# An expert stream fed in wider transfers: a loop over experts 4 to 29, and the drain for extra passes moved into their branch

## What is computed

```
g_prob  = softmax(xt @ w_group + b_group);  one group of 4
e_w     = the two best of the 8 experts of that group, renormalised
y       = (silu(xb @ w_gate[e]) * (xb @ w_up[e])) @ w_down[e]     for each of 32 experts, on its tokens
out     = sum over the two experts of each token of weight * y
```

## Time and profile before

| what | value |
|---|---|
| median of three runs | 1237.26 us |
| the profiled execution | 1237.28 us, span 1235.5 us |
| mixer and routing | until about 306 us |
| experts | 306 to 1218 us |
| TensorE busy | 931.6 us, 75% |
| DMA | 462.33 MB, mean 374 GB/s over the span |

### The profile page before, as it was taken

One profiled execution on the slowest core, in us unless ns is written; L12 is line 12 of the kernel. 1 busy time (PEld: TensorE's weight loads), 2 busy tenths in 40 slices (PEclk: granted clock), 3 DMA queues, 4 the chain that ended last, 5 costly groups with the idle time before them and its releaser, 6 DMA issues.

```text
span 1235.5 us, 17448 instructions
## 1 busy us (share of the span) xinstructions
PE 931.6 (75%) x7799; PEld 526.0 (43%) x7799; DVE 378.8 (31%) x480; ACT 223.3 (18%) x381; POOL 28.4 (2%) x60
## 2 busy tenths in 40 slices
PE   9999999999976666676666663866766766766774
PEld 7788788886433333333232321323333323323331
DVE  5454745444222222222222113222222222222214
ACT  6544555443100000000000000100000000000003
POOL 1100000000100000000000000000000000000003
PEclk9999999999988778878887876987788788787787
DMA  8877567858999999999999999999999999999993
GB/s 283 318 268 244 177 218 279 282 169 300 370 426 427 426 428 426 429 425 427 426 426 428 426 428 424 428 426 428 426 428 424 430 425 427 428 427 427 427 413 123
DMA packets 57083, 462.33 MB, mean 374 GB/s; under 512 B 5000, under 2 KB 5616, under 8 KB 31664
## 3 DMA queue, kind: packets, MB, share of 16 engines
q1 hardware_dynamic: 56272, 458.25, 90.7%
q0 software_dynamic: 656, 2.94, 0.7%
q10 hardware_dynamic: 80, 0.02, 0.0%
HBM read 459.09 MB, written 2.10 MB: 373 GB/s over the span
## 4 chain that ended last, share of the span: by engine, by line
DMA 55%; PE 40%; ACT 2%; DVE 2%; POOL 1%; issue 1%; POOLq 0%; ACTq 0%; DVEq 0%
DMA slot<-in_e_w_up 54%; PE scattered_out L1072 20%; PE bank L1261 8%; PE bank L1286 5%; PE bank L1234 2%; PE scattered_out L1299 1%; PE bank L1243 1%; ACT arena L594 1%; POOL h L426 1%; PE bank L1127 1%; DVE w_lo L693 0%; PE bank L1173 0%; ACT w_hi L440 0%; DVE acc L939 0%; DMA arena<-in_a_b_s 0%
## 5 line engine op out<-in xcount | busy, mean ns | idle before, releaser
L1261 PE MATMUL bank<-slot,arena 128*32 128x256 f32 x4064 | 340.4, 507 | 250.7 <-DMA slot<-in_e_w_up 249.5
L1261 PEld LDWEIGHTS bank<-slot,arena 128*32 128x32 f32 x4064 | 183.1, 144 | 417.4 <-issue 385.2
L939 DVE TENSOR_TENSOR acc<-scattered_out,acc 128x2048 f32<-128x2048 f32 x60 | 137.5, 2292 | 637.1 <-PE scattered_out L1299 637.1
L693 DVE TENSOR_TENSOR w_lo<-w_raw,w_hi 128x1024 fp32r<-128x1024 f32 x95 | 117.6, 1238 | 121.9 <-ACT w_hi L440 121.6
L440 ACT CAST w_hi<-w_raw 128x1024 fp32r<-128x1024 f32 x95 | 99.8, 1051 | 134.7 <-PE scattered_out L1072 128.2
L1072 PE MATMUL scattered_out<-w_hi,xT_first 128*128 128x512 f32 x376 | 122.8, 397 | 1.4 <-DVE w_lo L693 1.2
L1072 PE MATMUL scattered_out<-w_hi,xT_second 128*128 128x512 f32 x376 | 122.1, 396 | 0.5 <-DVE w_lo L693 0.5
L1286 PE MATMUL bank<-slot,arena 128*32 128x512 f32 x1024 | 118.2, 603 | 2.2 <-DVE arena L933 2.2
L604 ACT COPY arena<-bank 128x256 f32<-128x256 f32 x32 | 11.9, 372 | 562.5 <-PE bank L1261 562.5
L1072 PEld LDWEIGHTS scattered_out<-w_hi,xT_first 128*128 128x128 f32 x376 | 70.6, 188 | 19.7 <-DVE w_lo L693 3.4
L1072 PEld LDWEIGHTS scattered_out<-w_hi,xT_second 128*128 128x128 f32 x376 | 70.6, 188 | 17.0 <-DVE w_lo L693 0.9
(11 more groups left out here) (184 smaller groups left out, 432.2 us busy)
## 6 DMA issues: line engine op xcount, KB each, us to landing
slot<-in_e_w_gate SPq DMA_DIRECT2D x63, 2048.0 KB, 39.9
slot<-in_e_w_up SPq DMA_DIRECT2D x63, 2048.0 KB, 44.4
slot<-in_e_w_down SPq DMA_DIRECT2D x62, 2048.0 KB, 39.0
w_raw<-in_a_w_in SPq DMA_DIRECT2D x64, 512.0 KB, 3.9
w_raw<-in_a_w_out SPq DMA_DIRECT2D x32, 512.0 KB, 4.3
slot<-in_e_w_down SPq DMA_DIRECT2D x4, 1024.0 KB, 24.8
acc<-in_e_w_up SPq DMA_DIRECT2D x1, 2048.0 KB, 9.3
slot<-in_e_w_gate SPq DMA_DIRECT2D x2, 1024.0 KB, 10.2
```

The source lines that it names most:

```text
L693: dve.tensor_tensor(w_lo[:, hc % 2, :, :], w_raw[:, hc % 4, :, :], w_hi[:, hc % 2, :, :].bitcast(F32), ALU.subtract).then_inc(lo_done, 1)
L939: dve.tensor_tensor(acc[:, t, :], OUT[:, :], (acc if e else h)[:, t, :], ALU.add).then_inc(acc_done, 1)
L1261: ins = pe.matmul(GU[c * CAP:(c + 1) * CAP, 0:256], xeT[:, k % KC, 2 * a + k // KC, :], tiles[c // 2][:, k, (c % 2) * 256:(c % 2 + 1) * 25 ...
```

## The change

Experts 4 to 29 take gate and up in one 4 MB transfer each, 128 partitions by 32 KB, into two neighbouring slots; down stays in two of 2 MB. Chunks of experts 0 to 3, 30 and 31 stay at 2 MB, but a half of gate or up is now 16 KB out of each 32 KB row, so that the layout of rows is one for all; the gather's columns and the norm's `g_rows` follow it. Slots are given by a table instead of modulo ten. TensorE's instructions for these 26 experts are a loop of 13 turns over two experts, in which the waits are against values computed from the turn. SyncE, ScalarE and VectorE stay unrolled.

The break for extra passes is after expert 3, and nothing is drained there unless there is an extra pass: the drain, the list of passes and the renewal of the next expert's inputs are `flush` and `restore`, inside the branch.

```diff
+    LOOP, LAST_LOOP = 4, 30
+    SECOND_SLOTS, THIRD_SLOTS = (0, 2, 3, 4, 5, 6), (7, 8, 9, 1, 4, 5)
+    WIDE_SLOTS = ((2, 0), (7, 5))
+    EVEN_SLOTS, ODD_SLOTS = (2, 0, 3, 1, 4, 9), (7, 5, 8, 6, 4, 9)
-    BREAK = NEXP // 2
+    BREAK = LOOP
...
-                return w[0, e, a * D // 2:(a + 1) * D // 2, :].rearrange("(p k) n -> p k n", k=8)
+                return w[0, e].rearrange("(p a k) n -> a p k n", a=2, k=8)[a]
...
-        def extra_passes(eng, body):
+        def extra_passes(eng, flush, body, restore):
+            eng.wait_ge(extra_ready, 1)
             n = eng.value_load(n_extra_i[0:1, 0:1], min_val=0, max_val=MAXX)
             with eng.If(n > 0):
                 n_some = eng.value_load(n_extra_i[0:1, 0:1], min_val=1, max_val=MAXX)
+                flush()
                 with eng.Fori(0, n_some) as i:
                     body(i)
+                restore()
...
+            def load_wide(e, w):
+                sp.dma_start(wide_tile(e, w), (e_gate, e_up)[w][0, e].rearrange("(p k) n -> p k n", k=KD)
+                             ).then_inc(wide_in[e % 2][w], 16)
+            for i in range(IN_ACC + 4, NCH * LOOP):
+                load_when_free(i)
+            for e in range(LOOP, LAST_LOOP):
+                sp.wait_ge(gu_ps, e - 1)
+                if e == LOOP + 1:
+                    sp.wait_ge(gu_half, LOOP)
+                load_wide(e, 0)
+                if e == LOOP:
+                    sp.wait_ge(gu_ps, LOOP)
+                if e == LOOP + 1:
+                    sp.wait_ge(y_ps, LOOP)
+                load_wide(e, 1)
+                load_when_free(NCH * e + 4)
+                load_when_free(NCH * e + 5)
+            for e in range(LAST_LOOP, NEXP):
+                sp.wait_ge(gu_ps, e - 1)
+                for c in range(4):
+                    load_chunk(NCH * e + c)
+                sp.wait_ge(y_half, e)
+                load_chunk(NCH * e + 4)
+                sp.wait_ge(y_ps, e)
...
+                    if is_wide(NCH * e):
+                        tiles = [wide_tile(e, w)[:, 8 * a:8 * (a + 1), :] for w in range(2)]
+                        for w in range(2 if a == 0 else 0):
+                            pe.wait_ge(wide_in[e % 2][w], 16 * m + 16 * ((e - LOOP) // 2 + 1))
...
+            def looped_experts():
+                with pe.Fori(0, (LAST_LOOP - LOOP) // 2) as m:
+                    expert(LOOP, m)
+                    expert(LOOP + 1, m)
...
-            expert_run(0, BREAK)
-            pe.wait_ge(passes_ready, 1)
-            extra_passes(pe, extra_pass)
-            expert_run(BREAK, NEXP)
+            for e in range(BREAK):
+                expert(e)
+            extra_passes(pe, flush, extra_pass, restore)
+            looped_experts()
+            for e in range(LAST_LOOP, NEXP):
+                expert(e)
+            last_scatter(NEXP - 1)
```

More of the change, by code:

```diff
@@ L60, in sb @@
             return stack.enter_context(nc.sbuf_tensor(name, shape, dt))
-        slot = [sb(f"slot{i}", [P, 4096]) for i in range(5)]
+        low_slots = sb("low_slots", [P, 5 * 4096])
+        slot = [low_slots[:, i * 4096:(i + 1) * 4096] for i in range(5)]
         h = sb("h", [P, NT, D])
@@ L137, in hybrid_layer @@
             w_lo = sb("w_lo", [P, 2, 2, NBLK], F32R, mixer)
-        slot += [sb(f"slot{i}", [P, 4096]) for i in range(5, NSLOT)]
+        high_slots = sb("high_slots", [P, 5 * 4096])
+        slot += [high_slots[:, i * 4096:(i + 1) * 4096] for i in range(5)]
         acc = sb("acc", [P, NT, D])
@@ L615, in copy_y, with expert, flush @@
                 act.copy(y_sb, Y[:, :]).then_inc(y_ready, 1)
[L617 to L629, removed]
+            def expert(e):
+                copy_gu(e)
+                if e + 1 < NEXP:
+                    copy_xe(e + 1)
+                gate_silu(e)
+                if e == NEXP - 1:
+                    act.activation(unused[:, 3:4], eps_col[:, :], ACT.Sqrt)
+                copy_y(e)
+                if e + 1 < NEXP:
+                    copy_scatT(e + 1)
+            def flush():
+                act.wait_ge(passes_ready, 1)
             def extra_pass(i):
@@ L939, in add_out, with expert @@
                 dve.tensor_tensor(acc[:, t, :], OUT[:, :], (acc if e else h)[:, t, :], ALU.add).then_inc(acc_done, 1)
[L941 to L959, removed]
+            def expert(e):
+                if e > 0:
+                    add_out(e - 1, 0)
+                make_hT(e)
+                if e + 1 < NEXP:
+                    scale_xeT(e + 1)
+                if e + 2 < NEXP:
+                    choose(e + 2)
+                if e > 0:
+                    add_out(e - 1, 1)
             def list_passes():
-                dve.wait_ge(extra_ready, 1)
                 run = rx[:, RUN, :].unsqueeze(1).to_broadcast([P, MAXX, NEXP])
@@ L999, in extra_pass @@
                     dve.tensor_tensor(acc[:, t, :], OUT[:, :], acc[:, t, :], ALU.add).then_inc(x_add, 1)
[L1001 to L1004, removed]
+            choose(0)
+            dve.wait_ge(g_rows_in, 16)
+            scale_xeT(0)
+            choose(1)
+            for e in range(BREAK):
+                expert(e)
+            extra_passes(dve, flush, extra_pass, restore)
+            for e in range(BREAK, NEXP):
+                expert(e)
             def last_add(t, j):
@@ L1222, in _, with gather @@
             keep_busy(3)
-            def gather(e):
+            def gather(e, m=0):
                 if e == 0:
@@ L1310, in last_scatter, with expert @@
                                   start=True, stop=True).then_inc(scattered, 1)
[L1312 to L1333, removed]
+            def expert(e, m=0):
+                gate_up(e, m)
+                if e > 0:
+                    scatter(e - 1, 0, m)
+                if e + 1 < NEXP:
+                    gather(e + 1, m)
+                transpose_gu(e, m)
+                if e + 1 < NEXP:
+                    transpose_xe(e + 1, m)
+                if e == NEXP - 1:
+                    scatter(e - 1, 1, m)
+                down(e, m)
+                if 0 < e < NEXP - 1:
+                    scatter(e - 1, 1, m)
@@ new lines, in flush @@
+            def flush():
+                pe.wait_ge(passes_ready, 1)
+                pe.wait_ge(y_ready, BREAK)
+                pe.wait_ge(xeT_ready, BREAK + 1)
+                pe.wait_ge(scatT_ready, BREAK + 1)
+                for t in range(NT):
+                    if t == 0:
+                        pe.wait_ge(acc_done, NT * (BREAK - 1))
+                    else:
+                        pe.wait_ge(f_add, t)
+                    for j in range(NB):
+                        rows_j = slice(j * CAP, (j + 1) * CAP)
+                        ins = pe.matmul(O[j], scatT[rows_j, (BREAK - 1) % 2, t, :], y_sb[rows_j, :], start=True, stop=True)
+                    ins.then_inc(f_scattered, 1)
@@ new lines, in restore @@
+            def restore():
+                pe.wait_ge(r_sel, 1)
+                for t in range(NT):
+                    for j in range(NB):
+                        ins = pe.matmul(XE[j * CAP:(j + 1) * CAP, :], sel[:, BREAK % 2, t, :], gather_columns(t, j),
+                                        start=(t == 0), stop=(t == NT - 1))
+                ins.then_inc(r_xe_ps, 1)
+                pe.wait_ge(r_xe, 1)
+                for b in range(KC):
+                    ins = pe.transpose(TRX[:, b * P:(b + 1) * P], xe.rearrange("p (c k) -> p k c", k=KC)[:, b, :],
+                                       ident[:, :])
+                ins.then_inc(r_xeT_ps, 1)
+                for t in range(NT):
+                    ins = pe.transpose(XE[:, t * P:(t + 1) * P], scat[:, t, :, :].rearrange("p q c -> p (q c)"), ident[:, :])
+                ins.then_inc(r_scat_ps, 1)
+                pe.wait_ge(r_y, 1)
+                pe.wait_ge(r_xeT, 1)
+                pe.wait_ge(r_scatT, 1)
+                pe.wait_ge(r_next, 1)
@@ L1379, in _ @@
             pe.sem_inc(x_used, 1)
-            expert_run(0, BREAK)
-            pe.wait_ge(passes_ready, 1)
-            extra_passes(pe, extra_pass)
-            expert_run(BREAK, NEXP)
+            gather(0)
+            transpose_xe(0)
+            for e in range(BREAK):
+                expert(e)
+            extra_passes(pe, flush, extra_pass, restore)
+            looped_experts()
+            for e in range(LAST_LOOP, NEXP):
+                expert(e)
+            last_scatter(NEXP - 1)
 _INS = ["x", "norm_mix", "norm_ffn", "norm_final", "a_w_in", "a_ln_g", "a_ln_b", "a_w_s", "a_b_s", "a_w_out",
```

149 lines of the change are left out of this document (100 added, 49 removed).

## The result

The changed kernel takes 1224.69 us (1224.11 to 1227.15, 4 runs), the kernel before 1237.18. The ratio is 0.9902, 95% interval 0.989 to 0.9914; measured again on another occasion it was 1224.00 us and 0.9897 (0.988 to 0.9913).

A forecast was written before the change was run, and what follows sets the result against it. The prediction took the DMA stream's length on its slower half of engines, plus a fixed tail, to bound the kernel: 1237.28 - 4.6 (wider transfers) - 1.4 (TensorE's loop) = 1231.3 us, range 1227.5 to 1238.

The forecast's parts named there:

- What bounds: Whole kernel: the weight stream's length on the later-finishing eight of sixteen DMA engines, plus a fixed 33.5 us tail, sets the end.
- Fewer, wider transfers: Gate and up of 26 experts: 52 fewer transfers save 3.5 to 5.8 us; 4.6 us taken.
- the slower half's excess: Weight stream: on the eight later-finishing DMA engines a 2 MB chunk takes 4956 ns, 112 ns above its bytes.
- A loop on TensorE: TensorE's instructions for looped experts: 40 fewer fetch packets, bounds 0 and 2.8 us; 1.4 us less taken.
- more than packets: Rival, weight stream: wide transfers remove 5.8 us, instruction packets landing on the slower half alone 5.6 us; 1226 us, chance 0.10.
- Does the body stay: TensorE's loop: whether its 55 KB body of two experts stays with the engine or is fetched anew; even chance.
- Stops, computed waits, prefetch: Looped experts: a 7.5 us stop per turn fits 9 us of idle TensorE; the DMA queue never empties, margin 12 us.
- The switch and the break: Switch to wide transfers at expert 4, margin 14.6 us, costs nothing; removing the break's drain is worth 0.

## Why the prediction was wrong in size

**What bounds.** Right: the length of the stream, and of its slower half, plus a fixed tail (33.1 us for 33.5).

**Fewer, wider transfers.** Right in mechanism and size: 4.6 us forecast between 3.5 and 5.8, measured 5.1. The fixed time of a packet was worked out as 7.4 ns, and measured 9.3 and 10.5 ns; the upper bound, from the slower half, was 12.4. That the truth lies between the bounds is in part luck: about half of the slower half's excess, from which the upper one came, is not the rows' but the instruction packets' (52 on eight engines, 10 us over 181.5 chunks, 0.056 of the 0.112 us for one). A row of 32 KB is one packet, as assumed.

**A loop on TensorE.** This is the step that failed. It took 40 instruction packets at 0.070 us, by spreading q8's 0.4% share over all sixteen engines, put the outer bound at 2.8 us and chose 1.4. Measured: 7.2 us. The packets were counted right (38 went), their price was 2.7 times as high, 0.19 us. Two things make it so. They all fall on eight engines, which are the last to finish, and a landing waits for the last engine: without them the gap at the end shrinks from 9 to 2 or 3 us, with the wide transfers or without. And each costs its engine 1.56 us instead of 1.1, since it slows the packet behind it. The halving of 2.8 to 1.4, for the doubt whether the loop's body stays, took off another factor of two. The prediction had measured that gap and used it for the transfers, but not for this term. The rival "more than packets" had it (5.8 + 5.6 us, 1226), with a chance of 0.10. For that the single number that spoke for it, two halves that differ by 1%, was weighed too low. Why TensorE's packets go to eight engines, and why the packet behind one takes longer, stays open.

**Does the body stay.** The prediction gave an even chance to each. It does, at 55 KB and at 110 KB. The Trainium skill ("Runtime: NRT & Kernel Launch", Instruction fetch mechanics) has 128 KiB of instruction memory for TensorE and also says that a branch outside the present two pages of 16 KiB forces a fetch. The trace agrees with the first; the second does not hold for this backward branch, since no fetch came in the turns.

**Stops, computed waits, prefetch.** Right, and hidden as forecast. One expert of the changed kernel, its gate_up and then its issue of down for the next:

```profile
605.09 9.07 PE L1355 MATMUL bank<-high_slots,arena 128*32 128x256 f32 x128 [9.96 <-DMA high_slots<-in_e_w_up]
...
620.68 0.33 SPq L302 DMA_DIRECT2D low_slots<-in_e_w_down  x1
622.27 1.14 PE L1393 MATMUL scattered_out<-arena 32*128 32x512 f32 x8
622.40 0.33 SPq L302 DMA_DIRECT2D high_slots<-in_e_w_down  x1
```

With L at 605.0 the issues are at L + 15.7 and L + 17.4, inside the 15 to 17 and 17 to 19 forecast; TensorE waits 9.96 us for DMA before the block, and the longest stop within the expert is 0.27 us, for a copy of ScalarE. The queue never runs dry (share 1.00).

**The switch and the break.** Right: nothing at the switch to expert 4, where gate_up starts at 399.2 us (399.5 forecast), and nothing from the drain, which the run with both parts undone shows (0.9995).

## What to carry to other kernels

When a stream holds all DMA engines at a share of 1.00, look at how the share falls at its end: a step at 0.5 or 0.06 says that some engines are late, and whatever lands on these alone (instruction fetches first) costs the stream its time on an engine divided by their number, not by sixteen. An unrolled engine beside such a stream is a DMA load; a loop takes it away, and on TensorE a body of 110 KB still stays. Rows as long as the layout allows are worth about 10 ns per packet on each engine, even from 16 to 32 KB.

## What was not expected of the hardware

POOL's instructions come in packets of 8 KB on q14, on one DMA engine: 0.6 us of the stream each, so that 6760 instructions that do nothing of use on an otherwise idle engine made the kernel 32 us slower. (q14 is not POOL's alone: the changed kernel has 4 of its packets between 400 and 1150 us, where POOL executes nothing; whose they are no run shows.) TensorE's come in 16 KB on q8, in turn on eight engines, and cost 0.19 us each. Both slow the data packet behind them, by 0.49 us (q8) and 0.36 us (q14).
